# One chunk per half of the input projection, four filter spectra kept in SBUF, the decay-table products on VectorE

## The reference, cut to what matters

```python
mod = (silu(c) @ w_ada + b_ada)                    # 2048 -> 12288, split in six
sh1, sc1, g1, sh2, sc2, g2 = split(mod, 6)
h = x * (1.0 + sc1) + sh1
z = h @ w_in + b_in                                # 2048 -> 9216
z_u, z_v, z_h, z_g = split(z, [1024, 2048, 5120])
y_a = spatial_gating(gelu(z_u), gelu(z_v), ...) @ w_branch_a
y_b = hyena(z_h, ...) @ w_branch_b
mix = (gate_a * y_a + gate_b * y_b) @ w_o + b_o    # gates: sigmoid(z_g)
x = layer_norm(DEEPNORM_ALPHA * x + g1 * mix)

def hyena_filters(...):                            # h: 256 x 4096, from a small sine network
    return h.reshape(L, 2, 2, 1024) * window[:, None, None, :]      # the decay table
def hyena(z, ...):
    z = short_conv(z)                              # three taps
    v, x1, x2 = split(z, 3)
    for n, gate in enumerate((x1, x2)):            # two rounds
        y = gate * fft_long_conv(y, two_sided_spectrum(filt[:, 0, n], filt[:, 1, n]), skip[n])
```

## Time and profile before

| | |
|---|---|
| median of three runs | 2580.97 us |
| lowest, highest | 2577.54, 2586.88 us |
| profiled execution | 2574.01 us, span 2572.2 us |
| mean granted TensorE clock | 0.985 |

### The profile page before, as it was taken

How to read it: one execution, slowest core, us unless ns; L and a number is a source line. 1 busy time by engine, 2 the same in 40 slices (tenths; PEclk the granted TensorE clock), 3 DMA queues, 4 the chain that set the end, 5 groups by cost and what they waited for, 6 DMA issues and landing times.

```text
span 2572.2 us, 44652 instructions
## 1 busy us (share of the span) xinstructions
PE 2477.7 (96%) x17520; PEld 2323.6 (90%) x17520; DVE 1996.9 (78%) x2753; ACT 1382.4 (54%) x2163; POOL 854.5 (33%) x780
## 2 busy tenths in 40 slices
PE   6989999889988999999999989999999999999999
PEld 4989999889877888888888879999889999999998
DVE  7778789778899885556555669899877889888885
ACT  3445444343445554445544467777656676666663
POOL 2100020111145520001111229888103666666650
PEclk9999999999998999999999999999999999999999
DMA  9997577688985886555555534444454444444444
GB/s 356 367 354 239 188 240 249 209 306 291 326 279 196 285 281 212 189 180 198 188 196 189 187 117 164 165 149 161 172 186 163 155 156 156 156 149 155 149 156 148
DMA packets 148555, 537.63 MB, mean 209 GB/s; under 512 B 16967, under 2 KB 17912, under 8 KB 147832
## 3 DMA queue, kind: packets, MB, share of 16 engines
q1 hardware_dynamic: 144488, 521.12, 58.1%
q0 software_dynamic: 3856, 13.64, 1.5%
HBM read 528.40 MB, written 6.30 MB: 208 GB/s over the span
## 4 chain that ended last, share of the span: by engine, by line
PE 77%; DVE 7%; DMA 4%; issue 3%; POOL 1%; ACT 1%; DVEq 0%; POOLq 0%; ACTq 0%
PE ps L642 23%; PE ps L638 22%; PE ps L640 12%; PE ps L641 12%; DMA ring<-in_w_ada 4%; PE ps L980 3%; DVE wl L1072 2%; DVE ring L1090 1%; PE ps L675 1%; PE ps L884 1%; PE ps L990 1%; ACT wh L1827 1%; PE ps L722 0%; POOL misc L2541 0%; PE ps L635 0%
## 5 line engine op out<-in xcount | busy, mean ns | idle before, releaser
L1072 DVE TENSOR_TENSOR wl<-ring,wh 128x1024 fp32r<-128x1024 f32 x783 | 1031.0, 1328 | 368.0 <-ACT wh L1827 366.3
L642 PE MATMUL ps<-A,wl 128*128 128x256 f32 x4480 | 1269.9, 283 | 0.0
L640 PE MATMUL ps<-A,wh 128*128 128x256 f32 x3456 | 1006.7, 291 | 35.5 <-DVE A L1077 21.8
L1827 ACT CAST wh<-ring 128x1024 fp32r<-128x1024 f32 (+1 forms) x786 | 815.0, 1043 | 402.3 <-PE ps L642 317.8
L641 PE MATMUL ps<-A,wh 128*128 128x256 f32 x3456 | 982.2, 284 | 0.0
L642 PEld LDWEIGHTS ps<-A,wl 128*128 128x128 f32 x4480 | 861.1, 192 | 0.0
L640 PEld LDWEIGHTS ps<-A,wh 128*128 128x128 f32 x3456 | 666.8, 193 | 39.7 <-issue 18.4
L641 PEld LDWEIGHTS ps<-A,wh 128*128 128x128 f32 x3456 | 667.2, 193 | 1.4
L638 PE MATMUL ps<-B,wh 128*128 128x512 f32 x1696 | 597.3, 396 | 10.7 <-DVE wl L1072 6.4
L642 PE MATMUL ps<-B,wl 128*128 128x256 f32 x1696 | 475.8, 281 | 0.0
L638 PEld LDWEIGHTS ps<-B,wh 128*128 128x128 f32 x1696 | 318.6, 188 | 88.7 <-DVE wl L1072 9.4
(11 more groups left out here) (259 smaller groups left out, 2213.3 us busy)
## 6 DMA issues: line engine op xcount, KB each, us to landing
ring<-in_w_m SPq DMA_DIRECT2D x256, 512.0 KB, 4.4
ring<-in_hgrn_w_in SPq DMA_DIRECT2D x160, 512.0 KB, 3.6
ring<-in_w_ada SPq DMA_DIRECT2D x150, 512.0 KB, 5.4
ring<-in_w_in SPq DMA_DIRECT2D x144, 512.0 KB, 5.2
ring<-in_conv_w_in SPq DMA_DIRECT2D x96, 512.0 KB, 3.6
AF<-in_w_ada SPq DMA_DIRECT2D x42, 512.0 KB, 9.3
ring<-in_w_ab SPq DMA_DIRECT2D x32, 512.0 KB, 5.9
ring<-in_w_o SPq DMA_DIRECT2D x32, 512.0 KB, 6.1
```

Of the source, the lines that this page charges most:

```text
L640: e.matmul(dst, hi, x[:, 0, :], start=first, stop=False)
L642: return e.matmul(dst[:, 0:256], lo, x[:, 0, :], start=False, stop=last)
L1072: e.tensor_tensor(low[:, 0:k, :], ring[SLOT[h]][:, 0:k, :], hi[:, 0:k, :].bitcast(F32), ALU.subtract).then_inc(s.lo, 1)
L1827: e.copy(wh[h % NSPLIT][:, 0:k, :], ring[SLOT[h]][:, 0:k, :]).then_inc(s.hi, 1)
```

## The change

`chunks_at` becomes: in pass 1 one chunk per step up to h 31 and none behind; in pass 2 one at each odd step of the first 24 and one in four behind (15 in place of 4); in the last eight gate pairs one behind each half in place of two behind the pair; in `w_ab` 20 in place of 24, in `w_o` 17 in place of 20. VectorE's loops get a call of `chunks_behind` between the two halves of a pair. Chunks 48 to 63 take their slots in another order. Spectra 0 to 3 stay in `BF` and are read there by the hyena products; only 4 to 7 are spilled and read back, and `spectrum(7)` now stands behind `group(2)` and `group(3)`. All 16 products with the decay table, and `lo` of halves 0 to 2, are on VectorE. The spatial gating begins behind pair 40. The masks and the inverse transform's table are read at h 38 to 41 in place of h 20 to 28. `cond_early` is used for 76 chunks in place of 72.

```diff
-CHUNK_SLOT = [... else (1, 5, 6, 7)[j % 4] if j < 64
+CHUNK_SLOT = [... else (5, 6, 7, 1)[j % 4] if j < 64
 def chunks_at(h):
     if h < NB:
-        return 1
+        return int(h < 32)
     if h < 2 * NB:
-        return int(h < NB + 24 and (h - NB) % 6 == 5)
-    if h % 2 == 0:
-        return 0
+        return int((h - NB) % 2 == 1 if h < NB + 24 else (h - NB) % 4 == 3)
     if h < H_AB:
-        return 2 if h >= 128 else 1
+        return int(h % 2 == 1 or h >= 128)
     if h < H_WO:
-        return 1 + (h - H_AB) // 2 % 2
-    n = (h - H_WO) // 2
+        return int((h - H_AB) % 2 == 1 or (h - H_AB) % 8 == 6)
     if h < H_M1[0]:
-        return 1 + (n % 2 if n < 12 else 0) if n < 14 else 0
-    return 1
+        return int((h - H_WO) % 2 == 1 and h < H_WO + 30 or h - H_WO in (2, 6))
+    return h % 2
...
-    ksb = [BFf[:, 1024 * m:1024 * m + 1024] for m in range(4)]
-    ksb += [win[:, i, :] for i in range(2)] + [hw[:, i, 0:1024] for i in range(2)]
+    ksb = [BFf[:, 256 * a:256 * a + 1024] for a in (48, 52, 56, 60, 40, 24, 32, 16)]
...
             if 4 <= j < 12:
                 windowed(2 * (j - 4))
+                windowed(2 * (j - 4) + 1)
...
+            if j in (26, 28, 30):
+                lo(j // 2 - 13)
...
             for m in range(8):
+                k = ksb[m] if m < 4 else khat
+                kr, ki = two(k[:, 0:512]), two(k[:, 512:1024])
...
-                w.wait_ge(s.khat, 16 * m + 16)
+                if m < 4:
+                    w.wait_ge(s.spec, 2 * m + 2)
+                else:
+                    w.wait_ge(s.khat, 16 * m - 48)
...
             if sg:
                 next(sg, None)
+            chunks_behind(2 * i)
             lo(2 * i + 4)
             chunks_behind(2 * i + 1)
-            if i == 42:
+            if i == 40:
                 sg = spatial()
...
-        for n in range(8):
-            i = 2 * n + 1
-            w.wait_ge(s.fmm, 2 + i + 1)
-            e.copy(hw[:, 1, n * 512:n * 512 + 512], ps[3 + i % 3][:]).then_inc(s.fcp, 1)
...
-        for n in range(8):
-            x = hw[:, 1, n * 512:n * 512 + 512]
-            w.wait_ge(s.fcp, n + 1)
-            w.wait_ge(s.win, 16)
-            e.tensor_tensor(x, x, win[:, 1, n % 2 * 512:n % 2 * 512 + 512], ALU.mult).then_inc(s.early, 1)
         made_low(1)
-        for h in range(3):
-            w.wait_ge(s.hi, h + 1)
-            e.tensor_tensor(wl[h][:], ring[SLOT[h]][:], wh[h][:].bitcast(F32), ALU.subtract).then_inc(s.early, 1)
...
-            w.wait_ge(s.hv, HV * (m - 1) + 7)
+            w.wait_ge(s.hv, HV * (m - 1) + 7 if m > 4 else 0)
...
-        for m in range(4):
-            spectrum(m)
+        spectrum(4)
         for g in range(1, 4):
             sum_v(g)
         for g in range(4, 8):
             sum_v(g)
-        spectrum(4)
         group(0)
         group(1)
         for g in range(1, 8):
             sum_squares(g)
-        for m in range(5, 8):
-            spectrum(m)
-        for g in range(2, 8):
+        spectrum(5)
+        spectrum(6)
+        group(2)
+        group(3)
+        spectrum(7)
+        for g in range(4, 8):
             group(g)
```

More of the change, by code:

```diff
@@ L248 @@
     "lg rad rsq res "
-    "cre cst tap fcp early sigb cpad diag pt dt prod padd ta cy sgz silu gz gzp "
+    "cre cst tap sigb cpad diag pt dt prod padd ta cy sgz silu gz gzp "
     "lbd lbt lbm hg sm sp szs kk0 kk1 zz qq vi "
@@ L347, in cond_of @@
         half = CHUNKS[j][1]
-        if j < 72:
+        if j < 76:
             return cond_early[:, 1024 * half:1024 * half + 1024]
@@ L516, in wait_filters @@
     def wait_filters(w):
-        w.wait_ge(s.scr0, 64)
-        w.wait_ge(s.scr1, 64)
+        w.wait_ge(s.scr0, 32)
+        w.wait_ge(s.scr1, 32)
     def wait_lo(w, k, op):
@@ L558, in weights @@
             if BEFORE[h] is not None:
-                wait_split(w, BEFORE[h])
+                w.wait_ge(s.lo, BEFORE[h] + 1)
             elif SLOT[h] >= 4:
@@ L602, in sync_program @@
                 rows_in(2 + h // 14)
-            if h == 20:
+            if h == 38:
                 e.dma_start(dft[:, 4:6, :], d["k_dft"][:, 4:6, :]).then_inc(s.ident, 16)
                 e.dma_start(ident[:], d["k_ident"]).then_inc(s.ident, 16)
-            if h == 28:
+            if h == 41:
                 for k in range(8, 12):
@@ L645, in half @@
             hi, lo = wh[h % NSPLIT], wl[h % NSPLIT]
-            wait_split(w, h)
+            w.wait_ge(s.lo, h + 1)
             for k in ks:
@@ L655, in halves_by_turns @@
             for j in range(len(pbs)):
-                wait_split(w, h + j)
+                w.wait_ge(s.lo, h + j + 1)
             for k in range(8):
@@ L692, in tensor_program @@
         w.wait_ge(s.dft, 16)
-        w.wait_ge(s.fwin, 8)
-        w.wait_ge(s.fcp, 8)
-        w.wait_ge(s.early, 8)
+        w.wait_ge(s.fwin, 16)
         for i in range(16):
@@ L1191, in vector_program @@
                 windowed(2 * (j - 4))
+                windowed(2 * (j - 4) + 1)
             if j == 16:
                 first_bias(0)
-            if j in (23, 25, 27):
-                made_low((0, 2, 3)[(j - 23) // 2])
+            if j in (22, 23, 25):
+                made_low((0, 2, 3)[(22, 23, 25).index(j)])
+            if j in (26, 28, 30):
+                lo(j // 2 - 13)
         first_bias(1)
@@ L1215, in hyena @@
             two = lambda x: x.rearrange("p (m c) -> p m c", m=2)
-            kr, ki = two(khat[:, 0:512]), two(khat[:, 512:1024])
             real = strided(misc, 1536, (4136 - 1536, 2), (1, 256))
@@ L1340, in vector_program @@
                 taps(i - 1)
-            if i == 12:
+            if i == 18:
                 w.wait_ge(s.dft, 32)
@@ L1376, in vector_program @@
                 lo(H_AB + 2 * n + part + 3)
+                if part == 0:
+                    chunks_behind(H_AB + 2 * n)
             x, y = tmpA[2 * n % 4], tmpA[2 * n % 4 + 1]
@@ L1455, in vector_program @@
                 lo(H_WO + 2 * n + part + 3)
+                if part == 0:
+                    chunks_behind(H_WO + 2 * n)
                 if part == 0 and n == 15:
@@ L1894, in hyena @@
                 w.wait_ge(s.hv, HV * m)
-                w.wait_ge(s.chunk, 72)
+                w.wait_ge(s.chunk, 76)
                 w.wait_ge(s.cre, 16)
@@ L1926, in spilled @@
         def spilled(i):
-            if i < 16:
-                w.wait_ge((s.scr0, s.scr1)[i // 4 % 2], 16 * (i // 8) + 16)
-            elif i < 20:
-                w.wait_ge(s.scr0, 48)
-            elif i >= 32:
-                w.wait_ge(s.scr1, 48)
+            if i >= 16:
+                w.wait_ge(s.scr1, 16)
+            if i >= 24:
+                w.wait_ge(s.scr1, 32)
+            if i >= 32:
+                w.wait_ge(s.scr0, 16)
         def first_tap(j):
@@ L1982, in scalar_program @@
             wait_filters(w)
+            if n == ZG + 8:
+                w.wait_ge(s.hv, 4 * HV)
             if n == ZG + 24:
@@ L2383, in spill @@
             spilled[m % 2] += 16
-        spill(0, 28)
         made_low(4)
         made_low(7)
-        spill(1, 32)
-        spill(2, 36)
-        spill(3, 40)
-        spill(6, 43)
+        spill(7, 36)
+        spill(5, 40)
         made_low(10)
-        spill(7, 52)
+        spill(6, 48)
+        spill(4, 52)
         w.wait_ge(s.cre, 16)
@@ L2397, in gpsimd_program @@
         cond_again(cond_x[0], 0)
-        spill(4, 56)
-        spill(5, 60)
         made_low(13)
@@ L2455, in gpsimd_program @@
         w.wait_ge(s.hv, 8 * HV)
-        rows(0, 4, 128)
+        rows(0, 4, 64)
         w.wait_ge(s.cre, 48)
@@ L2468, in gpsimd_program @@
                 w.wait_ge(s.chunk, 128)
-                rows(4, 8, 144)
+                rows(4, 8, 80)
         w.wait_ge(s.gy, 32)
-        rows(8, 16, 160)
+        rows(8, 16, 96)
         total = Tally(s.sum)
```

14 lines of the change are left out of this document (4 added, 10 removed).

## The result

The changed kernel takes 2539.12 us (median of four runs, 2536.25 to 2548.81); the kernel before, run beside it, 2579.26 us (2576.31 to 2586.88). The ratio is 0.985, with a 95% interval of 0.981 to 0.988. The forecast was 2543 us in a range of 2524 to 2565.

What follows compares the result with a forecast made beforehand. TensorE, busy 96%, was taken as the bound, with only its waits to win. Gains summed to 37.8 us: 2574.0 profiled to 2536, stated as a 2543 us median because the profiled run lay 7 below it; range 2524 to 2565.

Steps and rivals of the forecast that it cites:

- Part 4: Pass 2: eleven more chunks put VectorE 1.4 us behind, within 5.7 us of slack; 0.5 us lost, bounds 0 and 5.
- Part 1: Ahead of pass 1: work moved from GpSimd to VectorE; start some 3 us later, then no stop; gain 1, bounds -1 and 3.
- the lock for whole instructions: Ahead of pass 1: VectorE and GpSimd exclude each other per instruction; each chunk would lose 0.68 us, 1.5 us more given back.
- three such: Ahead of pass 1: three chunks beside GpSimd's `lo`, 3.37 us each, 2.1 too long, would give 6.4 us back.
- Part 2: Middle of pass 1: chunk 48's slot free five steps ahead removes a 4.3 us wait and 2.4 of slow clock; gain 6.7.
- Part 3: Start of pass 2: chunks 64 to 67 gone, so TensorE's waits and slow clock go; gain 8.5 of 8.9, low end 5.
- Part 5: Gate pairs: group 2's wait and clock go, 10.1 us; VectorE's lateness swaps one wait for another, 0 net, bounds +2 and -5.
- Part 6: Last eight gate pairs: even dealing shortens landing to 5 us, cutting the 10.53 us wait; gain 6, bounds 1 and 10.
- Part 7: `w_ab` and `w_o`: seven chunks fewer, less VectorE lateness and fewer waits for `lo`; gain 6 us, bounds 2 and 8.
- Transfers take over: Rival, chance 0.18: pass 1 transfers need 95 us against TensorE's 99.3, waits for weights return, last-eight-pairs gain stays 1; 2553 us.
- VectorE takes over: Rival, chance 0.11: VectorE loses 5 us in pass 2 and 5 in the gate pairs; 2553 us.
- The slower case: Rival, chance 0.03: pass 2 lag passes 5.7 us, waits each pair keep the clock at 0.50; 2585 to 2627 us.

Runs made afterwards that it cites:

- the experiment: Kernel before with only the work ahead of pass 1 changed as after (decay-table products and `lo` of halves 0 to 2 on VectorE): 2584.76 us, ratio 0.998 to 1.002.
- the reverse edit: Kernel after with chunks 48 to 63 given their slots in the old order 1, 5, 6, 7 again: 2549.62 us, ratio to before 0.984 to 0.993.
- the last experiment: Kernel after with spatial gating begun at gate pair 42 and four slots for the last eight gate pairs' chunks: 2532.57 us, ratio to before 0.978 to 0.983.
- the doubled `lo`: Kernel after with VectorE's `lo` done twice at odd halves of pass 2, eleven times in the trace: 2560.45 us, ratio to before 0.989 to 0.993.
- the two groups of kernels: From `w_ab` to the first MLP matmul: four kernels dealing chunks there as before, 205.9 to 210.0 us; eight dealing as after, 200.4 to 201.6.

## Why the prediction was right, and where it was not

The kernel got faster by the mechanism forecast, at the places forecast, and by 33.6 us of the 37.8 summed. That the sum is so near is in part luck: Parts 5 and 6 together fell short by 8.4 us, and Parts 1, 2, 3, 4 and 7 gave 4.0 more than forecast. For each part I add up, over its stretch, what the spacing of TensorE's matmuls is above the usual, which takes a wait and its slow clock together:

| part | forecast | before lost | after lost | gain |
|---|---|---|---|---|
| 1, start of pass 1 | 1 | 4.5 + 1.6 | 2.35 later + 2.2 | 1.5 |
| 2, middle of pass 1 | 6.7 | 4.4 + 2.5 | 0 | 6.9 |
| 3, start of pass 2 | 8.5 | 2.9 + 2.4 + 2.9 + 1.9 | 0 | 10.1 |
| 4, pass 2 | -0.5 | 0 | 0 | 0 |
| 5, gate pairs | 10.1 | 0.7 + 2.0 + 1.6 + 8.5 + 2.0 | 1.1 + 2.5 + 2.4 + 1.4 | 7.4 |
| 6, last eight pairs | 6 | 1.0 + 0.6 + 10.7 + 1.5 | 0.4 + 0.7 + 10.5 + 1.8 | 0.3 |
| 7, `w_ab`, `w_o` (length) | 6 | 207.9 | 200.7 | 7.2 |

They sum to 33.4. Only Parts 1, 2, 5 and 6 had an experiment of their own, and Part 4 one on its margin. The gains of Parts 3 and 7, half of the total, are read from the traces of before and after: no run shows which of the edits they need.

**Part 1** was right, though two readings in its working were off. VectorE's rows of 20 to 41 us, which answer:

```profile
L1155 DVE TENSOR_TENSOR BF<-ps,BF 128x512 f32<-128x512 f32 x16 | 10.2, 680 | 0.0
L1077 DVE SCALAR_TENSOR_TENSOR AF<-AF,misc 128x1024 f32<-128x1024 f32 x8 | 9.6, 1213 | 1.5 <-DMA AF<-in_w_ada 1.5
```

A chunk takes 1.21 us. The 1.72 of the earlier trace rows is a mean over eight of which two were not slowed (1.22); the eight chunks that GpSimd's products slowed, two in `ring` among them, took 1.67 to 2.10 us, 1.84 on the mean. So 0.6 us each came back, 5 in all, and eight products more are paid for by that. The rows show how they were slowed. One of the eight, and the product of GpSimd that it met, before:

```profile
28.17 1.27 POOL L2370 TENSOR_TENSOR BF<-BF 128x512 f32<-128x512 f32 x1 [1.36 <-ACT BF L1863]
28.42 2.09 DVE L1090 SCALAR_TENSOR_TENSOR AF<-AF,misc 128x1024 f32<-128x1024 f32 x1
```

The product ends at 29.44 us and the chunk 1.08 us behind it, and so do all eight: each ends 1.08 us behind the end of the product that was running when it began. That looks as if a chunk begins its work only when the product is done, the lock for whole instructions that the prediction cites. But its reckoning from it was wrong twice: a product lasts 1.27 us and not 0.68, and a chunk loses only what is left of the product.

The 6.4 us for "three such" chunks were in truth two chunks (3.40 and 3.37 us) and a rest part (2.57 in place of 0.42); the sum is the same. The delay of the start was 2.4 us where 3 was said. What the prediction lacked is that the later start has an idle time of its own ahead of it, 4.36 us here, and the slow clock behind it. The gain of 1.5 is that of one execution, and the experiment does not show one by itself.

**Part 2** was right: 6.9 for 6.7, and the reverse edit brings the wait back. That its worth is 3.0 in one surrounding and 5.6 in another was not foreseen: a wait that is removed alone lets the next one grow.

**Part 3** was right in its places. It gained 10.1 us, 1.6 more than forecast: a wait costs 0.15 to 0.7 us more in the matmuls' spacing than its idle time says, and nothing was left over for the low end. Waits of 2.3 us and more stand there in all four kernels with the old chunks of pass 1 and 2; of the eight with the new ones only the last experiment has one of 1 us or more (1.18). That the chunks 64 to 67 alone did it is argued, not shown; the spills and the masks moved with them.

**Part 4** was right: no wait in pass 2, and the slack of 5.7 us that it relied on is borne out by the doubled `lo`. The margin is thinner than forecast, since a pair with a chunk takes VectorE 5.91 us against 5.75.

**Part 5** had the right mechanism and one wrong size. The 10.1 us for group 2 were there. "One wait for another, 0 net" was wrong: three waits, 6.0 us, stand for 2.0. Both also had slow clock behind one of them: the 16 matmuls behind the wait at 390 us took 3.47 us, those behind 1.97 us of waiting at 432 us, before, 3.68, and those at 357 us, at clock 1.00, 2.05. That makes 7.4 us for 3.6. VectorE in time order, after:

```profile
371.14 1.23 DVE L1059 TENSOR_TENSOR wl<-ring,wh 128x1024 fp32r<-128x1024 f32 x1 [3.58 <-ACT wh L1826]
...
377.64 0.69 DVE L1246 TENSOR_TENSOR misc<-misc 128x512 f32<-128x512 f32 x1
378.25 1.75 DVE L1273 RECIPROCAL statb<-statb 128x256 f32<-128x256 f32 x1
...
383.17 1.22 DVE L1059 TENSOR_TENSOR wl<-ring,wh 128x1024 fp32r<-128x1024 f32 x1
384.31 1.22 DVE L1077 SCALAR_TENSOR_TENSOR ring<-ring,XR 128x1024 f32<-128x1024 f32 x1
385.45 1.22 DVE L1059 TENSOR_TENSOR wl<-ring,wh 128x1024 fp32r<-128x1024 f32 x1
...
389.25 0.68 DVE L1255 TENSOR_TENSOR misc<-misc 128x512 f32<-128x512 f32 x1
```

VectorE idles 3.58 us for ScalarE just ahead of the crowded pairs, so it enters them with nothing in hand, and the reciprocal with its products (378.25 to 383.17) stands before the `lo` at 383.17 that TensorE wants at once. The prediction checked the lag only against the inverse transform, two halves on; `lo` was due sooner, and it waited there first (2.39) and at the transform again (2.35). The 1.07 us at 357 was not in the working at all. Two `lo` and a chunk between 344 and 354 us take 1.75 us instead of 1.22, each ending 1.08 us behind the end of one of GpSimd's sums of squares; with the start at pair 42 it is one `lo` and one chunk, and the wait is 0.71. So both fit together, but it was not tried apart.

**Part 6** was the step that failed: "Only the landing can get shorter ... If it is 5 us, the seven turns lose 5." The landing stayed at 5.5 us for the chunks of 485 to 545 us, the slots turned over in 6.9 us on the mean (5.9 to 8.1) where 7.0 was computed, and the wait stayed at 10.36. The sum of the turnover was right, the hope in the even order not; dealing the chunks out in twos changes nothing, and two places more take 10 us away. The low end, 1, was nearest to the 0.3 measured.

**Part 7** was right, 7.2 for 6: of the five waits for `lo`, 6.4 us, one of 0.2 is left. By the spread of the two groups of kernels it is 4 to 10 us.

**The rivals.** "Transfers take over" did not happen but was close: no wait in pass 1, and 3.6 us of them with 2.1 MB more. "VectorE takes over" came true for Part 5 by 4 of its 5 us and not for Part 4. The slower case needs a lag that passes the slack and a clock that falls behind short waits. Seven waits of 0.98 to 1.66 us did not do that. "Short waits (2.6) kept the clock at 1.00" was too strong, though: in the same trace the wait of 1.97 us at 432 us has 0.68 behind it, a row that the prediction did not read:

```profile
432.28:437.68 5.40, 5.40 (x33) 0.68 0.79 283
```

The forecast of the median, 2543, lies nearer to 2539 than its sum deserves: by the profiled executions it would be 2574.0 - 33.6 = 2540.4, for which 2536 was said. The forecast then added 7 us from the profiled execution to the median, where after's median lies 1.6 below its own profiled execution. So an error of 4.5 us was offset by one of 8.5 the other way.

## What to carry to other kernels

Divide a buffer's turnover (landing, use, issue) by its number of places and compare with the time in which one of its contents is wanted, before anything is done about order or bandwidth: 7.0 us in two places are 3.5 us a chunk, and two chunks a pair of 5.75 us want one every 2.9. That said all there was to say about the longest wait, and two places more took it away. When a crowded engine is given its work earlier, check the lag against everything it owes within the slack, and take the item that is due first. And take the parts of a change one at a time by a mark in the trace: of two edits made together in the gate pairs one won 10 us and the other lost 4.5. A part whose gain shows only where its edit does nothing, as with the work ahead of pass 1, has not been shown to gain.
